# Two transformer blocks on one core: gate evacuations moved ahead of the sparse attention's exponentials, first feed-forward units split by token tile

## What is computed

```python
h = x
u = rms_norm(h, norm_mix_pre)
z = u @ w_in                      # split into the inputs of four mixers
y_a = hgrn2_mixer(...)            # linear recurrence, chunks of 64
y_b = pool_mixer(...)             # trailing means
y_c = dsa_mixer(...)              # sparse attention: index scores, top 64 keys of each query
y_m = mem_attention(...)          # dense attention into 256 memory tokens
merged = sum(sigmoid(u @ w_gate[i]) * (y @ w_branch[i]) for i, y in enumerate((y_a, y_b, y_c, y_m)))
h = h + rms_norm(merged @ w_out, norm_mix_post)
u = rms_norm(h, norm_ffn_pre)
gt, up = split(u @ w_ffn_gate_up)                # D_FF = 2816 columns each
h = h + rms_norm((silu(gt) * up) @ w_ffn_down, norm_ffn_post)
```

## Time and profile before

| what | value |
|---|---|
| median of 3 runs | 1746.51 us (1745.61 to 1747.78) |
| the profiled execution | 1744.68 us, its span 1742.9 |
| TensorE busy | 1397.3 us, 80% |
| TensorE weight loads | 884.9 us, 51% |
| VectorE, ScalarE busy | 627.5 us (36%), 426.7 us (24%) |
| mean granted TensorE clock | 0.908 |

### The profile page before, as it was taken

How to read it: one execution, slowest core, us unless ns; L and a number is a source line. 1 busy time by engine, 2 the same in 40 slices (tenths; PEclk the granted TensorE clock), 3 DMA queues, 4 the chain that set the end, 5 groups by cost and what they waited for, 6 DMA issues and landing times.

```text
span 1742.9 us, 21660 instructions
## 1 busy us (share of the span) xinstructions
PE 1397.3 (80%) x8778; PEld 884.9 (51%) x8778; DVE 627.5 (36%) x1054; ACT 426.7 (24%) x615; POOL 0.7 (0%) x6
## 2 busy tenths in 40 slices
PE   8999999867566757766667666666799997989998
PEld 8789885522122212221222122212499997769997
DVE  5797944211001101110111011101377886444664
ACT  4455220201000000010000010000264846245543
POOL 0000000000000000000000000000000000000000
PEclk9999999988888888887887788888899998999999
DMA  9432546799999999999999999999743324555540
GB/s 362 163 146 98 204 184 249 290 428 429 429 428 428 428 430 429 428 428 430 429 428 428 429 429 429 428 428 430 307 167 104 139 98 169 188 185 173 192 169 24
DMA packets 64147, 530.73 MB, mean 305 GB/s; under 512 B 5698, under 2 KB 6978, under 8 KB 36308
## 3 DMA queue, kind: packets, MB, share of 16 engines
q1 hardware_dynamic: 64084, 529.86, 74.1%
HBM read 528.79 MB, written 1.05 MB: 304 GB/s over the span
## 4 chain that ended last, share of the span: by engine, by line
DMA 46%; PE 44%; DVE 6%; ACT 2%; issue 1%; DVEq 0%; SPq 0%; ACTq 0%
DMA shared<-in_w 25%; DMA ring<-in_w 21%; PE psum L363 9%; PE psum L445 7%; PE psum L446 7%; PE psum L447 7%; PE psum L1203 3%; PE psum L690 2%; PE psum L1227 2%; PE psum L1855 2%; DVE ring_parts L1570 1%; PE psum L549 1%; PE psum L1236 1%; PE psum L1651 1%; PE psum L1184 1%
## 5 line engine op out<-in xcount | busy, mean ns | idle before, releaser
L445 PE MATMUL psum<-parts 128*128 128x256 f32 (+1 forms) x744 | 227.2, 305 | 1.7 <-DVEq L2403 1.0
L446 PE MATMUL psum<-parts 128*128 128x256 f32 (+1 forms) x744 | 225.7, 303 | 0.0
L447 PE MATMUL psum<-parts 128*128 128x256 f32 (+1 forms) x744 | 225.7, 303 | 0.0
L1203 PE MATMUL psum<-shared,arena 128*32 128x512 f32 x1024 | 148.8, 713 | 78.0 <-DMA shared<-in_w 78.0
L1203 PE MATMUL psum<-ring,arena 128*32 128x512 f32 x1024 | 147.6, 711 | 70.1 <-DMA ring<-in_w 70.1
L1402 DVE TENSOR_TENSOR shared<-shared,psum 128x512 f32<-128x512 f32 x16 | 11.0, 687 | 457.4 <-PE psum L1203 457.4
L445 PEld LDWEIGHTS psum<-parts 128*128 128x128 f32 x744 | 143.0, 192 | 11.2 <-issue 4.9
L447 PEld LDWEIGHTS psum<-parts 128*128 128x128 f32 x744 | 143.0, 192 | 5.4
L446 PEld LDWEIGHTS psum<-parts 128*128 128x128 f32 x744 | 142.9, 192 | 5.2
L1227 PE MATMUL psum<-ring,shared 128*32 128x512 f32 x512 | 90.6, 844 | 64.6 <-DMA ring<-in_w 64.6
L1203 PEld LDWEIGHTS psum<-ring,arena 128*32 128x32 f32 x1024 | 32.7, 120 | 181.8 <-DMA ring<-in_w 116.5
(11 more groups left out here) (280 smaller groups left out, 1798.0 us busy)
## 6 DMA issues: line engine op xcount, KB each, us to landing
shared<-in_w SPq DMA_DIRECT2D x96, 2048.0 KB, 35.5
ring<-in_w SPq DMA_DIRECT2D x96, 2048.0 KB, 35.5
ring<-in_w_in SPq DMA_DIRECT2D x19, 2048.0 KB, 7.9
ring<-in_w_ffn_gate_up SPq DMA_DIRECT2D x11, 2048.0 KB, 8.0
ring<-in_w_gate SPq DMA_DIRECT2D x8, 2048.0 KB, 7.8
ring<-in_w_ffn_down SPq DMA_DIRECT2D x5, 2048.0 KB, 7.8
ring<-in_w_out SPq DMA_DIRECT2D x4, 2048.0 KB, 7.6
ring<-in_w_gla_out SPq DMA_DIRECT2D x2, 2048.0 KB, 7.9
```

Source lines behind the costliest of these rows:

```text
L445: pe.matmul(out, w[0], x[0], start=start, stop=False)
L446: pe.matmul(out, w[0], x[1], start=False, stop=False)
L447: return pe.matmul(out, w[1], x[0], start=False, stop=stop)
L1203: m = pe.matmul(ps[slots, bank, :], V.picked[:, k, slots], w[:, e, j, :], start=(k == 0), stop=(k == DT - 1))
```

## The change

It does three things. (1) The third evacuated gate of block two (gate0_4 to 7), with the high parts behind it, stands ahead of the sparse exponentials on ScalarE; the shares go from ScalarE to VectorE; VectorE makes gate2_0's low parts before and between the heads' maxima. (2) The rows after the output projection are taken tile by tile, and the first four feed-forward units run once for tile 0 and once for tile 1. (3) Tile 1's last four down units run over column half 0, then over column half 1.

```diff
 def second_pe
+    def up(n, tokens):
+        w = sp.shaped(n, 0), sp.shaped(n, 1)
+        for k in range(DT):
+            if n == 0 and k % 4 == 0:
+                pe.wait_ge(S("u_low"), tokens.start // P * 2 + k // 4 + 1)
+            m = three_passes(pe, ps[:, banks[n], tokens], [p[:, k, :] for p in w], [p[:, k, tokens] for p in sp.u],
+                             k == 0, k == DT - 1)
+        return m
     for t in range(TT):
         pe.wait_ge(S("u2"), t + 1)
         turn_rows(K, pe, B, "turn_u2", K.tiles(1, TT, D), t)
-    for n in range(UNITS_UP):
-        b = B.take(pe, f"ff{n}")
-        pe.wait_ge(S("unit_low"), n + 1)
...
+        for n in range(PART_BUFS):
+            if t == 0:
+                banks[n] = B.take(pe, f"ff{n}")
+                pe.wait_ge(S("unit_low"), n + 1)
+            m = up(n, slice(t * P, t * P + P))
+            if t:
+                m.then_inc(B.full[banks[n]], 1)
+    for n in range(PART_BUFS, UNITS_UP):
+        banks[n] = B.take(pe, f"ff{n}")
+        pe.wait_ge(S("unit_low"), n + 1)
+        up(n, slice(0, T)).then_inc(B.full[banks[n]], 1)
...
-    for f in range(FT - PART_BUFS, FT):
-        down_tile(f, 1)
+    for half in range(2):
+        for f in range(FT - PART_BUFS, FT):
+            down_tile(f, 1, (half,))
 def second_act
     gates(0, (0, 1, 2, 3))
+    gates(0, (4, 5, 6, 7))
+    act.preload_act_table_set("natural_log_exp_and_others")
     exps("ss", True)
-    gates(0, (4, 5, 6, 7))
-    shares("ss", 2)
+    act.preload_act_table(ACT.Sigmoid)
     gates(2, (0, 1, 2, 3))
...
+    for t in range(TT):
+        row_squares(t, 0)
+    mix_sd(0)      # squares of oz0_1 and the root
+    feed_sd(0)     # squares of h, tile 0, and the root
+    mix_sd(1)
+    u_high(0)      # high part of the transposed u2, tile 0
+    feed_sd(1)
+    u_high(1)
 def second_dve
     kept_mask()
-    largest("ss", True)
     lows(36, 38)
+    largest("ss", True, 0, 2)
+    lows(38, 39)
+    largest("ss", True, 2, 2)
+    lows(39, 40)
     inverse_sums("ss", True)
-    lows(38, 40)
+    shares("ss")
     merge(0)
...
+    mixed(0)       # gain, inverse root, h += z, tile 0
+    feed_rows(0)   # u2, tile 0
+    mixed(1)
+    u_low(0)       # low part of the transposed u2, tile 0
+    feed_rows(1)
+    u_low(1)
```

More of the change, by code:

```diff
@@ L86 @@
 STAT, NSTAT = columns(STAT_SIZES)
-ROW_SD = dict(ln1=0, ln2=TT, pre=2 * TT, post=3 * TT, ffn=4 * TT, last=5 * TT)
+ROW_SD = dict(ln1=0, ln2=TT, pre=2 * TT, post=3 * TT, last=5 * TT)
 CON, NCON = columns(CONST_SIZES)
@@ L1697, in scores, with turn_probs @@
         m.then_inc(B.full[b], 1)
-    def turn_probs(name, h, parts):
-        pe.wait_ge(S(f"{name}_done"), parts * (h + 1))
+    def turn_probs(name, h):
+        pe.wait_ge(S(f"{name}_done"), h + 1)
         b = B.take(pe, f"{name}_t{h}")
@@ L1775, in second_pe @@
     for h in range(AH):
-        turn_probs("ms", h, 1)
+        turn_probs("ms", h)
     split_tiles("gate3_0", (0, 1))
@@ L1838, in second_pe @@
     for h in range(AH):
-        turn_probs("ss", h, TT)
+        turn_probs("ss", h)
     for h in range(AH):
@@ L1858, in second_pe @@
         R.last_group[f"o{s}"] = f"oz1_{s}"
+    sp = Split(K)
+    banks = {}
+    def up(n, tokens):
[6 more added lines that the diff above has]
+        return m
     for t in range(TT):
@@ L1862, in second_pe, with down_tile @@
         turn_rows(K, pe, B, "turn_u2", K.tiles(1, TT, D), t)
-    sp = Split(K)
-    for n in range(UNITS_UP):
-        b = B.take(pe, f"ff{n}")
-        pe.wait_ge(S("unit_low"), n + 1)
[L1867 to L1872, removed]
+        for n in range(PART_BUFS):
[7 more added lines that the diff above has]
+        banks[n] = B.take(pe, f"ff{n}")
+        pe.wait_ge(S("unit_low"), n + 1)
+        up(n, slice(0, T)).then_inc(B.full[banks[n]], 1)
     down = {(t, half): B.take(pe, f"dn{t}_{half}") for t in range(TT) for half in range(2)}
-    def down_tile(f, t):
+    def down_tile(f, t, halves=(0, 1)):
         n = UNITS_UP + f
-        for half in range(2):
+        for half in halves:
             cols = slice(512 * half, 512 * half + 512)
@@ L1945, in exps @@
                     L.read(ins, B, f"{name}{h}")
[L1947 to L1953, removed]
     def turned_probs(name):
@@ L2069, in second_act, with row_squares, mix_sd, feed_sd @@
     scratch = K.A(10, 1024)
[L2070 to L2079, removed]
+    def row_squares(t, s):
+        b = B.wait_full(act, f"oz{t}_{s}")
+        L.done(act.activation(scratch[:, 0:512], ps[:, b, :], ACT.Square, accum_out=K.stat("squares", 2 * t + s)),
+               S("row_squares"))
+    def mix_sd(t):
+        row_squares(t, 1)
+        act.wait_ge(S("row_part"), t + 1)
+        L.done(act.activation(K.stat("sd", t), K.stat("squares", 2 * t + 1), ACT.Sqrt, bias=K.stat("part", t),
+                              scale=1.0 / D), S("row_sd"))
+    def feed_sd(t):
         act.wait_ge(S("h2"), t + 1)
-        L.done(act.activation(scratch, V.h[:, t, :], ACT.Square, accum_out=K.stat("squares", t)), S("row_squares"))
-        L.done(act.activation(K.stat("sd", t), K.stat("squares", t), ACT.Sqrt, bias=K.c("rms_eps"), scale=1.0 / D),
+        L.done(act.activation(scratch, V.h[:, t, :], ACT.Square, accum_out=K.stat("squares", 2 * t)), S("row_squares"))
+        L.done(act.activation(K.stat("sd", t), K.stat("squares", 2 * t), ACT.Sqrt, bias=K.c("rms_eps"), scale=1.0 / D),
                S("row_sd"))
-    for t in range(TT):
+    def u_high(t):
         for half in range(2):
@@ L2173, in second_dve, with largest @@
     lows(6, 8)
-    def largest(name, masked):
-        for h in range(AH):
+    def largest(name, masked, a=0, n=AH):
+        for h in range(a, a + n):
             b = B.wait_full(dve, f"{name}{h}")
@@ L2376, in second_dve, with gained, rstd, mixed @@
     K.wait_gain(dve, "n_ffn_pre")
[L2377 to L2392, removed]
-        L.done(dve.reciprocal(K.stat("rstd", t), K.stat("sd", t)), step)
+    def gained(t, s, squared):
+        b = B.wait_full(dve, f"oz{t}_{s}")
+        cols = slice(512 * s, 512 * s + 512)
+        dve.wait_ge(S("row_squares"), squared)
+        tt(z[:, t, cols], ps[:, b, :], K.gain("n_mix_post")[:, cols], ALU.mult)
+    def rstd(t, of):
+        dve.wait_ge(S("row_sd"), ROW_SD["post"] + 2 * t + of + 1)
+        L.done(dve.reciprocal(K.stat("rstd", t), K.stat("sd", t)), step)
+    def mixed(t):
+        gained(t, 1, 2 + TT + 2 * t + 1)
+        rstd(t, 0)
+        for half in range(2):
+            dve.sem_inc(B.free_of(f"oz{t}_{half}"), 1)
+        stt(V.h[:, t, :], z[:, t, :], K.stat("rstd", t), V.h[:, t, :], ALU.mult, ALU.add, S("h2"))
+    def feed_rows(t):
+        rstd(t, 1)
         stt(K.tiles(1, TT, D)[:, t, :], V.h[:, t, :], K.stat("rstd", t), K.gain("n_ffn_pre"), ALU.mult, ALU.mult, S("u2"))
-    for t in range(TT):
+    def u_low(t):
         for half in range(2):
@@ L2403, in second_dve @@
             dve.sem_inc(S("u_low"), 1)
+    for t in range(TT):
+        gained(t, 0, 2 + t + 1)
+        ts(K.stat("part", t), K.stat("squares", 2 * t), 1.0 / D, RMS_EPS, ALU.mult, ALU.add, S("row_part"))
+    mixed(0)
[4 more added lines that the diff above has]
+    u_low(1)
     for n in range(PART_BUFS, UNITS):
```

## The result

The changed kernel takes 1761.73 us (median of 4, 1761.01 to 1763.11) against 1746.80: a ratio of 1.0088, interval 1.0075 to 1.0101, some 15 us slower. Forecast was 1743.9 with a range to 1747.0. The first hole closed as forecast; the two passes of the first feed-forward units took 39.4 us (18.83 and 20.54) where 21.1 was put down for them: from 1.9 us into the first pass to the end of the second, TensorE ran at half its clock.

The account below looks back on a forecast made before the run. TensorE was taken as the bound from 1400 us on, apart from two large waits; -10.7 + 6.7 + 1.6 - 0.2 = -2.6 us, giving 1742.1 us profiled, 1743.9 against the median, range 1736.0 to 1747.0.

Parts of the forecast that it names:

- The first hole: TensorE's wait from 1460.12 to 1469.68 for gate2_0's first low part; forecast to shrink from 9.6 to 0.7 us.
- Part 1: Gate reordering around gate2_0: the branch starts at 1472.2 instead of 1482.9, worth -10.7 us, bounds -11.0 to -8.7.
- Rival (c): Gate2_1's late slab or the last minima hold the branch's banks or fourth unit; -0.6 us overall, 1745.9 us; chance 0.13.
- Part 2, when the pass starts: First feed-forward units: tile 0's first matmul at 1544.75 instead of 1549.97, a gain of 5.2 us there.
- The new wait before the second pass: Between the passes, tile 1's transposes and low part: 2.35 us in all, about 1.3 us of it a hole.
- the price of a 128-column product: In both passes, 0.110 us per load and matmul, set by the load; passes of 10.6 us, +6.7 us in all.
- The clock: At the hole before the first pass, granted clock falls to 0.50 for 3.41 us; transposes' 0.213 against 0.110 costs 1.6 us.
- Rival (b): The 192 split matmuls leave fp32r's fast form at 0.222 us each; whole +17.3 us, 1763.8 us; chance 0.10.
- The sign I had given, a distance of 0.22: In the two passes, a matmul distance of 0.06 or 0.22 us would show the forecast price wrong.
- (a): In the passes, the fp32r load is hidden and 128 columns cost about 0.060 us; whole -12.2, 1734.3 us; chance 0.17.
- Part 3: Last down units: only column half 1's product moves up, to 0.1 us behind the squares' end, worth -0.2 us.
- no wait of TensorE above 1 us between 1450 and 1540: Expected sign in the profile after, from gate2_0 to the output projection, that the large wait there was gone.

Follow-up runs that it names:

- the filled kernel: The changed kernel with the idle time before the first 128-column pass filled by seven plain fp32 products of 256 columns; median 1750.24 us, ratio 1.0017.
- mid-stream: The kernel before with feed-forward units 8 to 11 computed as two 128-column halves each, no hole near; 1756.74 us, ratio 1.0057.
- both holes filled: The changed kernel with the idle times before the first pass and between the two passes filled by plain fp32 products; median 1742.71 us, ratio 0.9980.
- parts 1 and 3: Kernel before with the gate reordering and the last four down units by column half, rows and first units unchanged; 1735.38 us, again 1735.28 us.
- part 1 alone: Kernel before with only gate0_4 to 7 ahead of the exponentials, shares on VectorE, low parts between maxima; 1737.25 us, ratio 0.9944.
- part 2 alone: Changed kernel with the gate reordering and the last units' column halves undone, keeping rows and first four units by token tile; 1774.69 us, ratio 1.0160.
- the rows by tile: Changed kernel with row work by tile but the first four feed-forward units whole over 256 columns; 1736.05 us, ratio 0.9943.
- the wide second pass: Changed kernel with the second pass over all 256 columns, tile 0's computed twice, first pass and its hole unchanged; 1754.87 us, ratio 1.0047.
- parts 1 and 3 with the hole before the transposes filled: parts 1 and 3 plus ten plain fp32 products of 256 columns in the 4.9 us hole before the transposes; 1736.85 us, ratio 0.9949.

## Why the prediction was wrong

**Part 1: right in size.** Forecast -10.7, in the trace -10.8; the run of it alone gave -9.4 (interval -12.6 to -6.8) and with part 3 -10.9 and -11.2. The order of events came out as worked out: bank first (0.5 us instead of 0.7), the fourth unit's low part in time, the late slab stopping ScalarE for 2.3 us and no bank of the branch. Rival (c) didn't happen.

**Part 2, when the pass starts: right.** First matmul at 1544.75 forecast; 1536.13 in the trace of after is 1544.7 on before's clock with the shift of 10.8 put back (+ 10.8 - 2.2). The new wait before the second pass came too, 0.8 us at half clock; I had 1.3.

**Part 2, the price of a 128-column product: right.** 0.110 forecast, 0.111 to 0.113 measured at full clock. In the filled kernel the two passes take 10.8 us each, so four split units cost 21.5 - 11.6 = +9.9 us; +10.1 was measured in mid-stream. With the 2.3 us between the passes there (2.35 forecast) and a gain of 5.3 (5.2 forecast) the forecast's +6.7 would have come out as +6.9.

**The clock: this step failed.** I wrote that the fall would cost 3.41 us at 0.213 instead of 0.110, "1.6 us". The fall came, as forecast, out of the first hole. What failed was to take its length from the kernel before, as if it were a fixed time: there 16 transposes ran in it, and the clock was back behind them. Here fp32r products of 128 columns followed, and with those the clock stayed at 0.50 until 256-column ones ran. The two passes took 39.4 us against the 21.5 of the filled kernel, 17.8 more; the wait and the transposes between them 2.7 instead of 2.3; the first four wide units 1.9 more than at full clock: 20.2 us in all, where 1.6 stood. -10.8 + 6.9 + 20.2 - 0.1 = +16.2, which is what was measured: the 18.4 between the spans less the 2.2 ahead of the change.

**Rival (b), near the figure for another reason.** It gave 1763.8 with 0.222 us a product, as a property of fp32r at 128 columns. The measured 0.214 comes near, but at full clock the same products take 0.112: the form isn't slow, the clock is. The sign I had given, a distance of 0.22, can't tell the two apart; the granted clock beside it does. (a) is refuted by the 0.112. The 81 ns that the Trainium skill ("TensorE: Matmul & The Clock Gate", Back-to-back issue gap) gives per load and matmul at 128 columns isn't seen at either clock. What the Trainium skill gives for the load alone ("TensorE: Matmul & The Clock Gate", LDWEIGHTS (loading the stationary operand)), the column count over 1.2 GHz, is 107 ns for 128 columns, near the 0.110 to 0.113 us at 2.4 GHz and half of the 0.214 us that a load and matmul took at 1.2 GHz.

**Part 3: right and unimportant.** The last product stands 0.2 us closer to the squares, the tail is 0.1 to 0.3 us shorter.

**Slips beside it.** 0.120 instead of 0.110 adds 1.9 to -2.6 and gives -0.7, not the -0.5 at the end of the forecast's own range. And the sign "no wait of TensorE above 1 us between 1450 and 1540" contradicts the forecast: part 1's 10.7 us move the hole that was to remain, 1541.4 to 1544.75, to 1530.7 to 1534.0, and there it was found (1532.74 to 1536.13 in after, less 2.24).

What stays open: why one execution in ten with both holes filled still lost 6 us; why fp32r products of 128 columns hold the half clock and transposes needn't; and what sets the moment of the fall. After the 4.9 us hole the half clock lasted 3.4 us in the kernel before, 6.8 in both runs of parts 1 and 3 and 10.2 in part 1 alone. Part of the difference lies in the hole itself: the clock fell 0.1 us behind the first transpose in the first, 2.8 and 2.4 us ahead of it in the others, where it cost nothing. Only in part 1 alone did it reach into the units, by 3.2 us.

## What to carry to other kernels

Before a product is split to fill a hole of TensorE, price the weight load: with 128x128 weights a matmul took 0.11 us with 128 columns as with one, and 0.12 with 256, so halving 256 columns nearly doubled the work (+9.9 us), and the closed hole bought back only half of that. Then ask what runs behind a hole that brings the clock down, and don't carry over the length of the half clock from a place where other work follows. Here fp32r products of 128 columns didn't lift it and 256-column ones did: put wide ones first, or keep TensorE at work through the hole. A row "busy 100%" says nothing of this; the granted clock and the distance of two matmuls do.

## What the runs showed of the hardware that I had not expected

- fp32r products of 128 columns ran at 1.2 GHz through 17.0 and 20.5 us of the changed kernel's two passes, TensorE shown busy without a break in each (the half clock lasted 44.4 us in all, there and with part 2 alone). Without a hole before them the same products ran at 2.4 GHz for 21.4 us. In these traces they held either level.
- 256-column products lifted the clock 2.3 to 4.1 us after the first of them wherever they ran at 0.50 (2.3 with part 2 alone, 2.9 with the rows by tile, 3.2 with part 1 alone, 3.4 with the wide second pass, 4.1 in the changed kernel). Transposes of 128 columns in plain float32 did so too in the kernel before (3.4 us) and in both runs of parts 1 and 3, but not with part 1 alone.
- At 1.2 GHz a load and matmul with 128 columns took 0.214 us, nearly twice the 0.112 at 2.4 GHz: what limits them slows with the clock.
- The clock can fall without a long hole: filled to 2.2 us of work in 4.9, with no wait above 1.6 us, it fell all the same (parts 1 and 3 with the hole before the transposes filled). That a hole of 1.2 us between the passes cost 8 us in some executions fits the times and is not shown by a trace.
